# Thirty-three stages of one program: an end of block between stages against waits by name

## What is computed

```
h = h + moba_attention(rms(h));   h = h + conv_ffn(rms(h))       # layer 1
h = h + rwkv7_time_mix(rms(h));   h = h + conv_ffn(rms(h))       # layer 2
h = rms(h)
k, v = mem @ mem_w_kv
for i in 0, 1:
    mix = differential_attention(h) if i == 0 else dsa_sparse_mla(h)
    h = layer_norm(alpha*h + mix)
    h = layer_norm(alpha*h + memory_cross_attention(h, k, v))
    h = layer_norm(alpha*h + hierarchical_moe(h))
```

## Time and profile before

| | us |
|---|---|
| median of 3 runs (lowest to highest) | 1787.18 (1785.92 to 1787.93) |
| the profiled execution's own time | 1789.54 |
| its span, first to last instruction | 1787.6 |
| its mean granted clock of TensorE | 0.984 |
| PE busy | 1697.0 (95% of the span) |
| DVE busy, ACT busy | 925.9, 693.4 |
| HBM read | 370.72 MB |

### The profile page before, as it was taken

One profiled execution on the slowest core, in us unless ns is written; L12 is line 12 of the kernel. 1 busy time (PEld: TensorE's weight loads), 2 busy tenths in 40 slices (PEclk: granted clock), 3 DMA queues, 4 the chain that ended last, 5 costly groups with the idle time before them and its releaser, 6 DMA issues. The chain is left out here.

```text
span 1787.6 us, 30705 instructions
## 1 busy us (share of the span) xinstructions
PE 1697.0 (95%) x12922; PEld 1323.4 (74%) x12922; DVE 925.9 (52%) x1954; ACT 693.4 (39%) x1317; POOL 0.2 (0%) x4
## 2 busy tenths in 40 slices
PE   8999999999999999999999999999978899999995
PEld 6789999786697799997877886555444788755552
DVE  6676556745366565575657663222123775522213
ACT  5475444323343444455555541111023464311111
POOL 0000000000000000000000000000000000000000
PEclk9999999999999999999999999999998999999998
DMA  8613444332201554435423347999943044499995
GB/s 323 236 71 142 157 197 165 114 142 103 76 4 73 187 212 158 173 142 188 179 105 113 147 169 319 425 424 426 426 199 115 15 169 172 189 420 425 424 425 215
DMA packets 36109, 373.81 MB, mean 209 GB/s; under 512 B 7024, under 2 KB 8176, under 8 KB 11392
## 3 DMA queue, kind: packets, MB, share of 16 engines
q1 hardware_dynamic: 33072, 366.18, 51.4%
q10 hardware_dynamic: 2896, 5.60, 0.9%
HBM read 370.72 MB, written 1.05 MB: 208 GB/s over the span
## 5 line engine op out<-in xcount | busy, mean ns | idle before, releaser
L2107 PE MATMUL ps<-ring,expert_inputs 128*64 128x256 f32 x2048 | 236.8, 384 | 8.8 <-DMA ring<-in_w_moe 8.7
L536 ACT CAST w_h<-ring 128x512 fp32r<-128x512 f32 x240 | 149.6, 626 | 143.3 <-PE ps L544 106.3
L539 DVE TENSOR_TENSOR w_l<-ring,w_h 128x512 fp32r<-128x512 f32 x240 | 163.5, 688 | 77.9 <-ACT w_h L536 74.1
L2107 PEld LDWEIGHTS ps<-ring,expert_inputs 128*64 128x64 f32 x2048 | 142.1, 137 | 79.5 <-DMA ring<-in_w_moe 10.0
L544 PE MATMUL ps<-ffn_x_h,ffn_w_h 128*128 128x256 f32 x704 | 199.7, 284 | 0.2
L544 PE MATMUL ps<-ffn_x_h,ffn_w_l 128*128 128x256 f32 x704 | 199.2, 283 | 0.0
L544 PE MATMUL ps<-ffn_x_l,ffn_w_h 128*128 128x256 f32 x704 | 199.2, 283 | 0.0
L539 DVE TENSOR_TENSOR ffn_w_l<-ring,ffn_w_h 128x1024 fp32r<-128x1024 f32 x132 | 155.6, 1219 | 19.7 <-ACT ffn_w_h L536 19.7
L536 ACT CAST ffn_w_h<-ring 128x1024 fp32r<-128x1024 f32 x132 | 131.5, 1046 | 53.0 <-PEq L1475 24.6
L544 PE MATMUL ps<-w_h,x_h 128*128 128x512 f32 x384 | 151.3, 394 | 0.2 <-DVE w_l L539 0.2
L544 PE MATMUL ps<-w_l,x_h 128*128 128x512 f32 x384 | 149.6, 390 | 0.0
(11 more groups left out here) (359 smaller groups left out, 2875.4 us busy)
## 6 DMA issues: line engine op xcount, KB each, us to landing
ring<-in_w_moe SPq DMA_DIRECT2D x64, 2048.0 KB, 14.9
ring<-in_w_proj SPq DMA_DIRECT2D x37, 2048.0 KB, 8.0
ring<-in_w_ffn SPq DMA_DIRECT2D x22, 3072.0 KB, 10.1
ring<-in_w_moe SPq DMA_DIRECT2D x64, 1024.0 KB, 15.7
ring<-in_w_b_in SPq DMA_DIRECT2D x1, 2496.0 KB, 19.4
ring<-in_w_lora SPq DMA_DIRECT2D x1, 2048.0 KB, 7.5
rows<-in_ln_g SPq DMA_DIRECT2D x4, 512.0 KB, 3.6
rows<-in_ln_b SPq DMA_DIRECT2D x4, 512.0 KB, 5.4
```

Of the source, the lines that this page charges most:

```text
L536: act.copy(high, x).then_inc(ready.up(), 1)
L539: return dve.tensor_tensor(low, x, high.bitcast(F32), ALU.subtract)
L2107: last = pe.matmul(bank(0)[g * SLOTS_E:(g + 1) * SLOTS_E, 0:2 * P], x[:, k, e * SLOTS_E:(e + 1) * SLOTS_E], wg[:, g, k, :], start=(k == 0) ...
```

## The change

All stages but the first run in two long blocks: one from the first projection to the RWKV features, one from the RWKV recurrence (`apart=True`) to the end. `new_block` returns the open block. A table `end` holds, for the stage in front, the semaphore and the count at which PE, ACT and DVE are done with what the next stage touches ("rows": at which its input is there), and each stage waits for the entries that it needs. `transpose_all` takes the jobs in another order and in other banks. The four fills at the start of `attention` go; the fills of the sub-norm move to bank 3. Row statistics and the norm's copies now count on semaphores. Cut to its core (stages of the same pattern are left out):

```diff
+        end, running, open_block = {}, [], ExitStack()
+        @contextmanager
+        def new_block(apart=False):
             for s in signals.values():
                 s.base = s.count
-            return nc.Block(no_gpsimd_drain=True)
+            if apart or not running:
+                close_block()
+                running.append(open_block.enter_context(nc.Block(no_gpsimd_drain=True)))
+            yield running[0]
+        def until(s, n=None):
+            return s.sem, s.count if n is None else s.at(n)
...
         def add_residual(dve, t, c, scale, product):
-            return row_stats(dve, t, c)
+            row_stats(dve, t, c).then_inc(sig("dve_step").up(), 1)
...
         def mean_squares(dve, x, first):
+            else:
+                dve.wait_ge(*until(sig("dve_step")))
...
         def norm(kind, gain, bias=None, z=None):
-                    fill(pe, 3)
+                    fill(pe, 3, end["bank"])
                     norm_pe(pe, norm, place, {1: 2, 3: 2, 5: 2, 7: 2})
                     fill(pe, 4)
+            end.update(act=until(from_act), dve=until(from_dve))
...
-        def transpose_all(pairs, scale=None):
+        def transpose_all(pairs, scale=None, late=False):
-                jobs = [(s, o, t, f) for s, o in pairs for t in range(T) for f in range(2)]
+                jobs = [(s, o, t, f) for f in range(2) for s, o in pairs for t in range(T)]
                 def _(pe):
+                    pe.wait_ge(*end["turned"])
                     for n, (s, o, t, f) in enumerate(jobs):
-                        if n >= 8:
-                            pe.wait_ge(free[n % 2].sem, free[n % 2].at(n // 2 - 3))
+                        if n == (0 if late else 4):
+                            pe.wait_ge(*end["act"])
-                            last = pe.transpose(bank(n % 8)[:, k * P:(k + 1) * P], s[:, t, c:c + P], ident[:])
+                            last = pe.transpose(bank((n + 4) % 8)[:, k * P:(k + 1) * P], s[:, t, c:c + P], ident[:])
+            end.update(pe=until(tp), act=until(free[0]), dve=until(free[1]))
...
@@ split_projection, ACT's list, ahead of its first cast @@
+                if "pe" in end:
+                    act.wait_ge(*end["pe"])
...
+        def open_rows(pe, norm):
+            if norm.kind == "rows":
+                for x in ("rows", "act", "dve"):
+                    pe.wait_ge(*end[x])
+                norm_pe(pe, norm, split_place, SPLIT_AFTER)
+            else:
+                fill(pe, 3, end["bank"])
+                norm_pe(pe, norm, split_place, SPLIT_AFTER)
+                fill(pe, 2, 0)
...
@@ project @@
+                rows_free = end.get("dve")
                 def load_rows(sp):
+                    if row_src:
+                        sp.wait_ge(*rows_free)
@@ project, dve_evac, behind a rotary part @@
+                        end["turned"] = until(sig("dve_step"))
@@ project, at its end @@
+            if residual is None:
+                end.update(pe=until(used), act=until(evac), dve=until(sig("weights_split")), rows=until(sig("weights_split")))
+            else:
+                end.update(pe=until(tail), dve=until(sig("dve_step")), bank=7)
...
@@ attention @@
                 def _(pe):
-                    fill(pe, 4)
+                    for x in ("act", "dve"):
+                        pe.wait_ge(*end[x])
+            end.update(pe=until(o_mm), act=until(pT_ready), dve=until(o_out), rows=until(o_out))
...
@@ ffn_stage @@
-                        fill(pe, 3, 0)
+                        fill(pe, 3, end["bank"])
+                        act.wait_ge(*end["pe"])
                         split_chunk(0, 0)
+                end.update(pe=until(summed), dve=until(sig("dve_step")), bank=0)
+                if ahead:
+                    end.update(rows=until(ahead_in), act=until(sig("hidden_high")))
...
@@ rwkv, features, DVE's list @@
+                    for x in ("act", "dve"):
+                        dve.wait_ge(*end[x])
@@ rwkv, recurrence @@
-            with new_block() as block:
+            with new_block(apart=True) as block:
...
@@ differential, sub-norm: PE, then ACT @@
-                    fill(pe, 14)
+                    fill(pe, 14, 3)
+                    act.wait_ge(*end["dve"])
...
@@ mixture: PE, then SP @@
-                    fill(pe, 3)
+                    fill(pe, 3, end["bank"])
                 def _(sp):
+                    sp.wait_ge(*end["pe"])
...
@@ sparse_mla, up-projection, PE @@
+                    pe.wait_ge(*end["dve"])
-                                if n >= 8:
-                                    pe.wait_ge(ev.sem, ev.at(n - 7))
+                                if n == 6:
+                                    pe.wait_ge(*end["act"])
-            transpose_all([(q_tok, qT), (qi_tok, qiT)])
+            end.update(act=until(ev), turned=until(sig("dve_step")))
+            transpose_all([(q_tok, qT), (qi_tok, qiT)], late=True)
@@ sparse_mla, index scores, PE @@
+                    for x in ("act", "dve"):
+                        pe.wait_ge(*end[x])
+            end.update(act=until(ev))
```

More of the change, by code:

```diff
@@ L419, in _ @@
                         if bias is None:
-                            act.activation(xT[:, k, :], place(k), ACT.Copy, scale=gain[:, k:k + 1])
+                            act.activation(xT[:, k, :], place(k), ACT.Copy, scale=gain[:, k:k + 1]).then_inc(from_act.up(), 1)
                         else:
-                            act.activation(xT[:, k, :], place(k), ACT.Identity, bias=bias[:, k:k + 1], scale=gain[:, k:k + 1])
+                            act.activation(xT[:, k, :], place(k), ACT.Identity, bias=bias[:, k:k + 1], scale=gain[:, k:k + 1]).then_inc(from_act.up(), 1)
                 @block.vector
@@ L654, in _ @@
                 def _(pe):
[L655 to L659, removed]
-                        fill(pe, 3, 0)
-                        norm_pe(pe, norm, split_place, SPLIT_AFTER)
-                        fill(pe, 2, 0)
+                    open_rows(pe, norm)
                     def rows_of(q, t):
@@ L890, in _ @@
                                 act.activation(x, x, ACT.Exp, bias=nmax[:, b, t:t + 1], scale=-1.0 if masked else 1.0, accum_out=sums[:, b, t:t + 1]).then_inc(p_ready.up(), 1)
+            end.update(pe=until(o_mm), act=until(pT_ready), dve=until(o_out), rows=until(o_out))
+        end["bank"] = 0
         mask_in, x_in, ident_in, cols_in = sig("mask_loaded"), [sig(f"x_loaded{t}") for t in range(T)], sig("identity_loaded"), sig("columns_loaded")
@@ L1815, in _ @@
                         load(sp, j)
+            end.update(pe=until(out_done), dve=until(sig("dve_step")), bank=6)
         memK, memV = fm(0), tok(1)
@@ L1880, in _ @@
                     link(dve, "dve_step", dve.tensor_tensor(o3, o3, stat[:, 32:48].rearrange("p (a o) -> p a o", o=1).broadcast_to([P, 16, P]), ALU.mult))
+            end.update(dve=until(sig("dve_step")), rows=until(sig("dve_step")), act=until(sig("row_root")))
             project(2, residual=ALPHA, row_src=(d["ln_g"][0], d["ln_b"][0]), norm=from_rows(o, stat[:, 48:49]))
@@ L2455, in _ @@
                         act.copy(kT[96:128, hd, :], bank(6)[96:128, 0:SEQ])
-                    act.copy(kiT, bank(6)[:, SEQ:2 * SEQ])
+                    act.copy(kiT, bank(6)[:, SEQ:2 * SEQ]).then_inc(ev.up(), 1)
                 @block.vector
@@ L2487, in _ @@
                             g3 = col(g, 0, 2).rearrange("p (k o) -> p k o", o=1).broadcast_to([P, 2, P])
-                            dve.tensor_tensor(cT[:, 2 * a:2 * a + 2, t * P:(t + 1) * P], bank(4 + t)[:, a * 256:(a + 1) * 256].rearrange("p (k s) -> p k s", k=2), g3, ALU.mult)
+                            dve.tensor_tensor(cT[:, 2 * a:2 * a + 2, t * P:(t + 1) * P], bank(4 + t)[:, a * 256:(a + 1) * 256].rearrange("p (k s) -> p k s", k=2), g3, ALU.mult).then_inc(dv.up(), 1)
                 stream(block, 1)
+            end.update(act=until(ev), dve=until(dv))
             j0 = next_unit(2)
```

18 lines of the change are left out of this document (11 added, 7 removed).

## The result

| | before | after |
|---|---|---|
| median (lowest to highest), us | 1786.55 (1783.89 to 1787.93), 4 runs | 1757.18 (1756.04 to 1757.83), 4 runs |
| the profiled execution: time, span, clock | 1789.54, 1787.6, 0.984 | 1756.04, 1754.2, 0.985 |

The ratio is 0.9837, 95% interval 0.982 to 0.9854: 29.4 us less between the medians. The forecast was 28.7 less, 1758.5. The two profiled executions lie 33.5 apart, more than the medians; the rest comes in the main from how the two executions began, which experiment 8 shows.

A forecast was written before the change was run, and what follows sets the result against it. PE (TensorE), busy 95% of the span, was taken as the bound of a chain of 33 stages. Terms 7.4 + 4.1 + 2.7 + 3.5 + 4.7 + 1.1 + 2.4 + 1.8 + 1.0 = 28.7 us off 1787.2: 1758.5 us, range 1752 to 1770.

The forecast's parts named there:

- transposes and attention, two places: Four starts, transposes and scores at two attentions: new bank order and no fills bring scores 3.7 us earlier, twice, 7.4.
- cross attentions: Two cross attentions: scores start right behind ACT's copies, without meeting or fills, 2.05 us earlier each, 4.1 together.
- MLA up-projection: PE waits for DVE's cT alone, for ACT's small copies only at the seventh bank: 2.7 us.
- top-k to attention: Third masked attention: three maps' scores run beside DVE's top-k and the mask step needs only DVE: 3.5 us.
- seven norm starts: Starts with a norm of h: DVE follows its own statistics, 0.6 us each, plus 0.25 twice in feed-forward stages: 4.7.
- six row starts: PE's transposes from token rows, behind five attentions' outputs and at the memory keys: 0.4 us each, 2.4.
- bare meetings: Six meetings on the path, such as projections behind projections, MLA transposes and final norm: 0.3 us each, 1.8.
- norm behind the mixture and the start behind it: First mixture: ACT's table load comes early, up to 1.25 us and 0.3; colder array possible; 1.0 taken of 0 to 1.6.
- The clock rival: Without fills each of five attentions gets a half-clock stretch costing 1.65 us, 8 in all: 1766.5 us; chance 0.15.
- Attentions at half clock from end to end: Slower rival: five attentions run wholly at half clock, up to 90 us more, 1848 us; chance 0.03.
- Bare meetings only: Waits by name end no sooner than meetings, so each start gives its bare 0.3: 9 us, 1778 us; chance 0.07.
- No change, by code fetches of the single block: The same engines are last by name, or the single block brings its own code fetches: 1787 us; chance 0.03.

The follow-up runs named there:

- experiment 8: The changed kernel run again unaltered beside the others: median 1759.19 us of five; once more, 1758.72 us.
- experiment 5: Changed kernel with more fills at the sub-norm, the top-k and the MLA down-projection, none added behind the mixtures: 1754.56 us; repeated, 1753.98 us.
- experiment 1: Changed kernel with an end of block behind every stage again, waits by name, new transpose order and missing fills kept: 1784.69 us, ratio 0.9989.
- experiment 3: Changed kernel with one meeting put back, ahead of the MLA up-projection alone: 1760.20 us in one execution.
- experiment 6: Changed kernel whose two transposes of 36 heads again wait for ACT's banks before their first jobs: 1761.0 us in one execution.
- experiment 4: Changed kernel with more fills behind the mixtures, in the sub-norm, in two MLA down-projection waits and beside the top-k: 1756.89 us.
- experiment 2: Changed kernel with the four fills again at the start of each attention, behind its waits: 1765.11 us, ratio 0.9884.

## Why the prediction was right, point by point

| term | forecast | measured as steps |
|---|---|---|
| transposes and attention, two places | 3.7 each | 3.80 (1.63 and 2.17) and 3.82 (1.65 and 2.17) |
| cross attentions | 2.05 each | 2.11 each |
| MLA up-projection | 2.7 | 2.90 |
| top-k to attention | 3.5 (2.9 to 4.5) | 1.86 (2.10 with the next start's 0.24); 4.49 at full clock |
| seven norm starts | 4.7 | 0.65 to 0.69 at five, 0.88 and 0.89 at two: 5.1, less 1.5 of half clock at one |
| RWKV mixing | 1.1 | 1.12 |
| six row starts | 0.4 each | 0.13 or 0.14 at the three attentions that can be read alone, 0.24 behind the top-k, 0.54 at the memory keys |
| bare meetings | 0.3 each | 0.24 to 0.30 |
| norm behind the mixture and the start behind it | 1.0 | 0.90 and 0.18 in experiment 5, where the mixture in front has the same half clock as before; 3.73 and 1.13 in the changed kernel, with the mixture's clock |

**The starts** are right to a few tenths, because each was read from the row of the engine that would be last by name, and not from the idle time of the engine that waited. Experiment 1 shows that the waits by name carry them, all but some 2 us of it, experiment 3 the same at one place alone, and experiment 6 the share of the order of the banks.

**Top-k** was mis-sized: 1.86, below its whole range of 2.9 to 4.5. The half clock took not "up to 1.65" but 2.6. The mechanism stands (DVE follows its mask at once). The step that failed is the sentence that PE's "next few microseconds run at half clock as now (3.30 us)": it was 6.80. The idle time ahead doesn't explain it, for it is 4.63 now and was 5.46 before, ahead of the four fills at 1408.90. Six more fills give back the 2.6 in both profiles of experiment 5, and 1.0 in experiment 4; the four fills of experiment 2 halve the stretch and give 1.0. That the missing fills are part of it is therefore shown; why the stretch is twice as long behind a shorter idle time is open.

**Row starts** were taken at 0.4, though the rows gave 114.95 for 115.2. PE now starts 0.14 behind DVE's last division (108.14 to 108.28) where it took 0.39, and DVE's own last step comes 0.1 later in the stage. Some 0.8 us too much over three places.

**The clock** is where the total was helped by luck. The mean stayed (0.984, 0.985), as foreseen. But by place it moved, between these two profiles. Lost: a new half stretch at the sub-norm's projection (1.5) and a longer one at the top-k (2.6 in place of up to 1.65). Won: one stretch of 3.4 fewer in the RWKV (three between 428 and 470 before, two after; a step of 1.65 that no term has), less in the MLA's down- and up-projection (13.6 before, 10.2 after), and none in the first mixture, where the kernel before had 6.8. With this one and one of 3.4 fewer behind it, the two starts behind the mixture measure 4.9 for the 1.0 that was forecast. Against the forecast the top-k, the sub-norm and the row starts fell short by 1.6, 1.5 and some 0.8, and the mixture and the RWKV gave 3.9 and 1.65 more. So that the sum came out within 0.7 of the measured 29.4 is partly chance; the starts by themselves are right. Nothing here shows why the mixture's stretch comes and goes.

**The rivals.** The clock rival does not happen at four of the attentions in the changed kernel's profiles, where PE's idle time ahead of the scores is 0.88 to 1.16; at the fifth, behind the top-k, it does. With the meetings back it happens at a cross attention (1.90 idle, experiment 1). And it can happen at the others: in the profile of experiment 4 the first attention, whose code is the changed kernel's, has half clock from 89.0 to 92.4 and gives back 1.6, just the rival's price of 1.65. The Trainium skill ("TensorE: Matmul & The Clock Gate", "HAM oscillation") says idle gaps between matmuls are to be kept short or the clock falls; the traces agree in direction, and the runs add that behind idle times of 0.88 and 1.16 ahead of the scores the clock stayed, and behind 1.90 (experiment 1) and 4.63 it fell. Behind the 2.45 ahead of the output projection's transposes it fell in four profiles and stayed in two (experiments 2 and 6), and where longer fills leave 0.72 it stayed in all three. But behind 1.13 (experiment 1) and 0.73 (second profile of experiment 5) ahead of the first output projection's transposes it fell. So a gap's length alone does not tell. Attentions at half clock from end to end: none. Bare meetings only (1778, 9 us): with all fills in place the waits by name still give 21.4 (experiment 2), and one meeting alone costs 2.99 (experiment 3). No change, by code fetches of the single block: the single block brings none of its own (queue q8 has 106 instruction fetches before and after). But one that was hidden behind a meeting now sets when PE's fills start behind the first mixture (experiment 4); the norm's chain runs as long there, so it costs little.

The marks named ahead: no line 148 between 509 and 841 (so it is); scores 4.5 behind the last projection matmul (82.32 - 77.56 - 0.23 = 4.5); the sequencer at two places (two); line 2555 within 0.2 of 2535's end (0.05); line 876 within 0.3 of the mask (0.13); line 309 within 0.1 (it starts 0.03 to 0.04 behind its statistics at all norms). The last mark, that a new wait of over 1 us ahead of lines 364 or 841 would show it wrong, was touched at two kinds of place though the forecast held. At the cross attentions PE waits 1.16, which holds ACT's two copies; before, it waited 1.5 at the meeting, ahead of the fills. Ahead of the sub-norm's output projection it waits 2.45 for 1.67, as its fourteen fills now start and end earlier.

## What to carry to other kernels

A meeting of all engines costs its bare 0.3 us only where the last engine is the one whose result is needed; otherwise it costs the distance between the two, 3 us at one place here. Read, for each stage, which product the first instruction needs and when that is there, and price the change as that difference. Fills that hold a clock are worth their time ahead of a wait (0.4 for four) and cost all of it behind one (1.9), and they cover a gap only if PE issues them when the gap begins (4.98 late in experiment 4, behind an instruction fetch); after every change of the gaps their number has to be set again, place by place, and by several executions, since half clock that goes at one place came at another (6.5 us gained at three places, 3.6 in the medians).

## What was not expected of the hardware

The same first 16 transposes took 3.67 us in one execution and 1.97 in another, by when the clock first rose; that alone is 3 us between two profiles of one program, and a window over a stretch ahead of the clock's record shows 1.00. PE's first matmuls behind the mixture's branch start 2.54 to 2.57 us behind an instruction fetch of 16 KB, 4.8 to 5.2 behind the matmul before them, with no wait in the program. And an idle time of 1.90 us without fills behind it, shorter than the 5.40 of the earlier trace rows, was enough to be followed by half clock (24 scores in 7.11 for 5.34).
